# Third tile's gates: half by packed indirect adds, half by one-hot products; alternating heads; single gathers

## The reference, cut to what matters

```python
q = (xb @ w_query).reshape(T, PEER_HEADS, 2, PEER_HALF)             # 8 heads
s = einsum('thpk,hpnk->thpn', q, sub_keys)                          # 2 x 128 sub keys
top_s, top_i = top_k(s, 16)
cand_s = top_s[:, :, 0, :, None] + top_s[:, :, 1, None, :]
cand_i = top_i[:, :, 0, :, None] * 128 + top_i[:, :, 1, None, :]
best_s, best_pos = top_k(cand_s.reshape(T, 8, 256), 16)
idx = take_along_axis(cand_i.reshape(T, 8, 256), best_pos)          # 8 x 16 experts a token
gate = softmax(best_s)
act = gelu(einsum('td,thkd->thk', xb, expert_u[idx]))
out = einsum('thk,thkd->td', gate * act, expert_v[idx])
```

## Time and profile before

| | us |
|---|---|
| median of 3 runs | 2357.9 |
| lowest and highest | 2355.63, 2358.73 |
| profiled execution | 2360.8 |
| its span, first to last instruction | 2359.0 |
| busy: PE | 2306.6 |
| busy: DVE | 1470.8 |
| busy: ACT | 911.8 |
| busy: POOL | 779.1 |

### The profile page before, as it was taken

One profiled execution on the slowest core, in us unless ns is written; L12 is line 12 of the kernel. 1 busy time (PEld: TensorE's weight loads), 2 busy tenths in 40 slices (PEclk: granted clock), 3 DMA queues, 4 the chain that ended last, 5 costly groups with the idle time before them and its releaser, 6 DMA issues.

```text
span 2359.0 us, 29706 instructions
## 1 busy us (share of the span) xinstructions
PE 2306.6 (98%) x11108; PEld 1932.5 (82%) x11108; DVE 1470.8 (62%) x2879; ACT 911.8 (39%) x1342; POOL 779.1 (33%) x624
## 2 busy tenths in 40 slices
PE   8989899999999999999999999999999999999998
PEld 7879888888887888788888888888888788888887
DVE  4276568777435767667896553222222688888887
ACT  5346544333325445433333443222223333333333
POOL 0030011211000000000087777778630665656540
PEclk9999999999999999999999999999999999999999
DMA  6212057885222222333466558766666899999993
GB/s 231 82 45 63 1 166 237 291 275 192 98 98 85 86 72 63 119 103 101 125 137 159 121 121 226 193 143 145 147 210 217 288 369 370 373 379 378 356 391 107
DMA packets 205596, 434.21 MB, mean 184 GB/s; under 512 B 54176, under 2 KB 104368, under 8 KB 205072
## 3 DMA queue, kind: packets, MB, share of 16 engines
q1 hardware_dynamic: 81840, 251.79, 31.1%
q0 software_dynamic: 72848, 119.73, 18.7%
q10 hardware_dynamic: 50768, 60.82, 7.7%
HBM read 369.22 MB, written 63.05 MB: 183 GB/s over the span
## 4 chain that ended last, share of the span: by engine, by line
PE 94%; DVE 3%; ACT 1%; issue 1%; another core or an unknown queue 0%; DMA 0%; POOL 0%; ACTq 0%; DVEq 0%; POOLq 0%
PE PS L281 28%; PE PS L283 28%; PE PS L282 28%; PE PS L2346 1%; PE PS L2464 1%; PE PS L2278 1%; PE PS L2198 1%; PE PS L2266 1%; PE PS L2442 1%; PE PS L2123 1%; PE PS L2132 0%; DVE WL L276 0%; PE PS L2094 0%; PE PS L2232 0%
## 5 line engine op out<-in xcount | busy, mean ns | idle before, releaser
L276 DVE TENSOR_TENSOR WL<-RAW,WH 128x1024 fp32r<-128x1024 f32 (+1 forms) x414 | 505.4, 1222 | 687.3 <-ACT WH L270 658.6
L281 PE MATMUL PS<-HH,WH 128*128 128x512 f32 x1696 | 667.4, 394 | 6.5 <-DVE HL L513 4.6
L283 PE MATMUL PS<-HH,WL 128*128 128x512 f32 x1696 | 660.8, 390 | 0.0
L282 PE MATMUL PS<-HL,WH 128*128 128x512 f32 x1696 | 660.7, 390 | 0.0
L270 ACT ACTIVATE WH<-RAW 128x1024 fp32r<-128x1024 f32 (+1 forms) x414 | 435.6, 1054 | 445.8 <-PE PS L283 350.3
L942 POOL DMA_INDIRECT gates<-A,PLACE x256 | 420.2, 1641 | 316.6 <-DVE PLACE L1907 186.2
L281 PEld LDWEIGHTS PS<-HH,WH 128*128 128x128 f32 x1696 | 318.9, 188 | 75.1 <-issue 6.5
L283 PEld LDWEIGHTS PS<-HH,WL 128*128 128x128 f32 x1696 | 318.7, 188 | 67.0
L282 PEld LDWEIGHTS PS<-HL,WH 128*128 128x128 f32 x1696 | 318.9, 188 | 65.0 <-issue 1.0
L281 PE MATMUL PS<-WH,WGH 128*128 128x512 f32 x768 | 300.0, 391 | 2.1 <-DVE WGL L1968 1.0
L283 PE MATMUL PS<-WH,WGL 128*128 128x512 f32 x768 | 299.6, 390 | 2.4 <-issue 2.4
(11 more groups left out here) (375 smaller groups left out, 2640.1 us busy)
## 6 DMA issues: line engine op xcount, KB each, us to landing
RAW<-in_peer_u SPq DMA_DIRECT2D x128, 512.0 KB
RAW<-in_peer_v SPq DMA_DIRECT2D x128, 512.0 KB
A<-in_w_ada POOLq DMA_DIRECT2D x48, 512.0 KB, 4.8
A<-gates ACTq DMA_DIRECT2D x32, 768.0 KB
A<-acts ACTq DMA_DIRECT2D x32, 768.0 KB
RAW<-in_ffn_up SPq DMA_DIRECT2D x44, 512.0 KB
gates<-A POOLq DMA_DIRECT2D x16, 1024.0 KB, 6.9
acts<-GATE SPq DMA_DIRECT2D x64, 256.0 KB
```

The lines of the kernel that those rows point to most:

```text
L276: nc.vector.tensor_tensor(WLr[:, slot(c), 0:w], RAW[:, slot(c), 0:w], WH[:, slot(c), 0:w], ALU.subtract).then_inc(sem("low_done"), 1)
L281: nc.tensor.matmul(out, L[0], R[0], start=first, stop=False)
L282: nc.tensor.matmul(out, L[0], R[1], start=False, stop=False)
L283: return nc.tensor.matmul(out, L[1], R[0], start=False, stop=last)
```

## The change

`PACKED = 64` tokens of tile 2 now take the way of the adds, 64 that of the one-hot products.

- Tile 2 also gets addresses (`THIRD`) and gates. POOL packs them by four small DMAs from 64 partitions x 128 picks to 128 partitions x 64 picks (partition p + 64 holds the second eight picks of each head of token p), waits for them, and needs 64 indirect adds of 128 addresses for these 64 tokens. So there are 320 adds instead of 256. The zeroed columns grow from 256 to 320 (`ZW`).
- One-hot groups fall from 16 to 8 (`NG8`), and the staging tile and its store to half.
- Heads of tile 0, 1 and 2 alternate: tile 1 starts two rounds after tile 0, the packed half two rounds after tile 1. The packing stands before the fifth round.
- ACT's wait for the adds and its first loads of gates move from `QU - 6` to `QU - 3`, and include the third count.
- In the last stage POOL gathers 12 activations first and then one activation behind each row, five picks ahead; `final_w` is loaded at the 33rd row.
- SP stores the last activations one behind each of the first seven `peer_v` loads, instead of three so and four together.
- In two of the norms `root_of_rows` of tile 2 comes after the last tile's second half.
- Some semaphores are merged under other names.

```diff
+PACKED = P // 2
+ZW = NP * P + PACKED
+NG8 = (P - PACKED) // 8
...
+ACTS_AHEAD = 5
...
                 first_half(link, PS[:, 2 * t, :], 0)
-                root_of_rows(act, link, tag, 2)
                 rows_multiplied(act, tag, t + 1)
                 second_half(link, PS[:, 2 * t + 1, :], 0, product_sq[:, t:t + 1], product_rstd[:, t:t + 1], "product_root")
+                root_of_rows(act, link, tag, 2)
...
                 load((c0 + QU + v, 0, 0), peer_v[v])
-                if v < 3:
+                if v < 7:
                     keep_acts(P - 7 + v)
-                if v == 3:
-                    for k in range(P - 4, P):
-                        keep_acts(k)
...
-            for t in range(NP):
-                pool.wait_ge(sem("gates_listed"), t + 1)
-                for u in range(PICKS):
-                    if u >= TOPK and u % TOPK == 0:
-                        pool.wait_ge(sem(f"gates_placed{t}"), 16 * u)
-                    pool.indirect_dma_start(out=gate_list, out_offset=bass.IndirectOffsetOnAxis(ap=PLACE[:, t, u:u + 1], axis=0),
-                                            in_=SHARES[:, t, u:u + 1], in_offset=None, compute_op=ALU.add)\
+            def pack():
+                pool.wait_ge(sem("gates_listed"), NP + 1)
+                for dst, src in ((PACKED_AT, THIRD), (PACKED_SHARES, SHARES[:, NP])):
+                    for half in range(2):
+                        ps = slice(PACKED * half, PACKED * half + PACKED)
+                        pool.dma_start(dst[ps, :].rearrange("p (h k) -> p h k", h=PH),
+                                       src[0:PACKED, :].rearrange("p (h k) -> p h k", h=PH)[:, :, 8 * half:8 * half + 8])\
+                            .then_inc(sem("picks_packed"), 16)
+                pool.wait_ge(sem("picks_packed"), 64)
+
+            def add_head(t, h):
+                n, at, shares = (TOPK, PLACE[:, t], SHARES[:, t]) if t < NP else (TOPK // 2, PACKED_AT, PACKED_SHARES)
+                if h == 0 and t < NP:
+                    pool.wait_ge(sem("gates_listed"), t + 1)
+                if h > 0:
+                    pool.wait_ge(sem(f"gates_placed{t}"), 16 * n * h)
+                for u in range(n * h, n * h + n):
+                    pool.indirect_dma_start(out=gate_list, out_offset=bass.IndirectOffsetOnAxis(ap=at[:, u:u + 1], axis=0),
+                                            in_=shares[:, u:u + 1], in_offset=None, compute_op=ALU.add)\
                         .then_inc(sem(f"gates_placed{t}"), 16)
+
+            for r in range(PH + 4):
+                if r == 4:
+                    pack()
+                for t in range(NP + 1):
+                    if 0 <= r - 2 * t < PH:
+                        add_head(t, r - 2 * t)
...
-            pick_acts(0)
-            pool.dma_start(ROW[:, :], dr["final_w"].partition_broadcast(P)).then_inc(sem("row_landed"), 16)
-            pick_acts(1)
+            for u in range(SLOTS + ACTS_AHEAD):
+                pick_act(u)
             for u in range(SLOTS, PICKS):
                 pick_row(u)
-                if u % 8 == 7 and u // 8 + 2 < PICKS // 8:
-                    pick_acts(u // 8 + 2)
+                if u + ACTS_AHEAD < PICKS:
+                    pick_act(u + ACTS_AHEAD)
+                if u == PICKS // 4:
+                    pool.dma_start(ROW[:, :], dr["final_w"].partition_broadcast(P)).then_inc(sem("row_landed"), 16)
...
-                if p == QU - 6:
+                if p == QU - 3:
                     for t in range(NP):
                         act.wait_ge(sem(f"gates_placed{t}"), 16 * PICKS)
+                    act.wait_ge(sem(f"gates_placed{NP}"), 16 * PICKS // 2)
...
                 token = con("token")[:, t:t + 1].to_broadcast([P, PICKS])
-                if t < NP:
-                    nc.vector.scalar_tensor_tensor(PLACE[:, t], EXPERT, float(DW), token, ALU.mult, ALU.add)\
+                if t < ND:
+                    place = PLACE[:, t] if t < NP else THIRD
+                    nc.vector.scalar_tensor_tensor(place, EXPERT, float(DW), token, ALU.mult, ALU.add)\
                         .then_inc(sem("gates_listed"), 1)
...
-                for c in range(8 * n, 8 * n + 8):
+                for c in range(PACKED + 8 * n, PACKED + 8 * n + 8):
```

More of the change, by code:

```diff
@@ L51 @@
 NP = ND - 1
-ZW = NP * P
-NG8 = P // 8
+PACKED = P // 2
+ZW = NP * P + PACKED
+NG8 = (P - PACKED) // 8
 PICKS = PH * TOPK
@@ L778, in build @@
         SHARES = A[:, 21760:22144].rearrange("p (t u) -> p t u", t=ND)
-        STG = A[:, 0:16384].rearrange("p (i t) -> p i t", i=P)
+        STG = A[:, 0:8192].rearrange("p (i t) -> p i t", i=P)
+        THIRD = over("A", "THIRD", 8192, PICKS, U32)
+        PACKED_AT = over("A", "PACKED_AT", 8320, PICKS // 2, U32)
+        PACKED_SHARES = A[:, 8384:8448]
         OHA = A[:, 16384:18432].rearrange("p (r n) -> p r n", r=16)
@@ L951, in pick_row, with pick_act @@
                     .then_inc(sem(f"row_picked{u % SLOTS}"), 16)
[L953 to L961, removed]
+            def pick_act(u):
+                if u % 8 == 0:
+                    wait(pool, "rows_summed", u - 15)
+                pool.indirect_dma_start(out=AG[:, u:u + 1], out_offset=None, in_=act_list,
+                                        in_offset=bass.IndirectOffsetOnAxis(ap=A_AT[:, u:u + 1], axis=0))\
+                    .then_inc(sem(f"acts_picked{u // 8 % 2}"), 16)
+            pool.wait_ge(sem("gates_listed"), NT)
             pool.wait_ge(sem("gates_stored"), 16)
@@ L1079, in _ @@
                     act.wait_ge(sem("maxima_taken_off"), 1)
-                    nc.scalar.activation(E4, E4, ACT.Exp).then_inc(sem("late_exp"), 1)
+                    nc.scalar.activation(E4, E4, ACT.Exp).then_inc(sem("exps_taken"), 1)
                     act.wait_ge(sem("maxima_taken_off"), 2)
-                    nc.scalar.activation(lbt[:, 4:12], lbt[:, 4:12], ACT.Exp).then_inc(sem("late_exp"), 1)
+                    nc.scalar.activation(lbt[:, 4:12], lbt[:, 4:12], ACT.Exp).then_inc(sem("exps_taken"), 1)
                 if s - 1 in PTC_AT:
@@ L1279, in _ @@
                         act.wait_ge(sem("maxima_taken_off"), 2 + t + 1)
-                        nc.scalar.activation(BV[:, t % 2], BV[:, t % 2], ACT.Exp).then_inc(sem("best_exp"), 1)
+                        nc.scalar.activation(BV[:, t % 2], BV[:, t % 2], ACT.Exp).then_inc(sem("exps_taken"), 1)
                 if p == LIST_AT:
@@ L1562, in _ @@
                 if s == 27:
-                    dve.wait_ge(sem("late_exp"), 1)
+                    dve.wait_ge(sem("exps_taken"), 1)
                     for t in range(NT):
@@ L1573, in _ @@
                 if s == 29:
-                    dve.wait_ge(sem("late_exp"), 2)
+                    dve.wait_ge(sem("exps_taken"), 2)
                     link(nc.vector.tensor_tensor(lbt[:, 0:4], lbt[:, 4:8], lbt[:, 8:12], ALU.add))
@@ L1893, in listed @@
             def listed(t):
-                dve.wait_ge(sem("best_exp"), t + 1)
+                dve.wait_ge(sem("exps_taken"), 2 + t + 1)
                 n1, n2 = N12[:, t % 2, 0], N12[:, t % 2, 1]
@@ L1902, in listed @@
                     last.then_inc(sem("list_ready"), 1)
-                    return
                 link(nc.vector.scalar_tensor_tensor(EXPERT, n2, float(P), n1, ALU.mult, ALU.add))
                 token = con("token")[:, t:t + 1].to_broadcast([P, PICKS])
-                if t < NP:
-                    nc.vector.scalar_tensor_tensor(PLACE[:, t], EXPERT, float(DW), token, ALU.mult, ALU.add)\
+                if t < ND:
+                    place = PLACE[:, t] if t < NP else THIRD
+                    nc.vector.scalar_tensor_tensor(place, EXPERT, float(DW), token, ALU.mult, ALU.add)\
                         .then_inc(sem("gates_listed"), 1)
@@ L1911, in listed @@
                     nc.vector.scalar_tensor_tensor(V_AT, n1, float(P), n2, ALU.mult, ALU.add)\
-                        .then_inc(sem("picks_listed"), 1)
+                        .then_inc(sem("gates_listed"), 1)
             def shifted(t):
```

## The result

| | before | after |
|---|---|---|
| median, us (7 runs each) | 2358.04 | 2367.23 |
| lowest and highest | 2355.63, 2361.98 | 2363.07, 2373.31 |
| profiled execution, us | 2360.8 | 2363.07 |
| its span | 2359.0 | 2360.8 |

The ratio is 1.0032 with a 95% interval of 1.0021 to 1.0044: slower, by 5 to 10 us. The forecast was 2379.1: the right side and inside the range, but +21 where +9 was measured.

What follows compares the result with a forecast made beforehand. PE was taken to bound the kernel, with POOL's longer add stream delaying the last stage: +25.9 + 3.4 - 6.8 - 1.3 = +21.2 us on the median of 2357.9 gives 2379.1, range 2347 to 2412.

Steps and rivals of the forecast that it cites:

- T: Theory tested by the runs: the end of POOL's adds sets the start of the last stage, one to one.
- VectorE's missing wait: Sign in the norm transitions: no 0.66 us wait before VectorE's line 462 in the trace after.
- the period of 1.99: Sign in POOL's stream: 320 adds with a mean period near 1.99 us; under 1.92 the prediction is wrong.
- One-hot products: PE in the query stage: 8 of 16 one-hot groups go, at 1.78 us each, -14.2 us.
- The stream: POOL's indirect adds in the query stage: 320 x 1.990 = 636.8 us, plus 12 for landing waits and 10 for packing.
- Rival (c): POOL's stream: landing waits hid the gaps, so alternating heads gains nothing; +40 us more, 2419; chance 0.12.
- Rival (b): POOL's stream: VectorE stretches the adds, fewer one-hot rows speed them; 29 us less, -8, 2350; chance 0.08.
- Landing and loads: Start of the last stage: last add lands 3.0 us after its end, then 12 us of loads until PE starts.
- +25.9: PE's start of the last stage moves from 1821.0 to 1846.9 us, the 14.2 saved on one-hot products included.
- Restart: PE at the start of the last stage: reduced clock after standing for 40 us, +3.4 us.
- Single gathers: POOL in the last stage: one act beside each row spreads the gathers and removes the stall near 1862, -6.8 us.
- The norms: Transitions at 351 and 730 us: squares before tile 2's root_of_rows remove VectorE's wait, -1.3 us.

Runs made afterwards that it cites:

- e3: Changed kernel with 32 of its 64 packed adds left out, so its output is incomplete: 2339.03 us, 0.9937 of before.
- e7: Changed kernel with its tiles' adds one tile after the other instead of alternating heads: 2415.38 us, 1.0257 of before.
- e4: Changed kernel with 32 instead of 64 tokens by packed adds, 96 by one-hot products: 2346.41 us, 0.9967 of before.
- e1: Kernel before, unedited, run again for a second trace: 2352.76 us.
- e6: Kernel before with only the change's last-stage POOL order (single activation gathers, later final_w load): 2354.46 us, 0.9994 of before.
- e5: Kernel before with only the heads of its two tiles alternating: 2357.91 us in one execution.
- e8: Changed kernel with POOL's seven first row gathers held until the first group of activations landed: 2362.7 us, 1.0029 of before.
- e2: Changed kernel, unedited, measured and traced again: 2366.5 us, 1.0046 of before.
- e9: Changed kernel with reordered heads, a later wait for packing, row gathers held back and first row sum two chunks later: 2345.99 us, 0.9954 of before.

## Why the prediction was right and wrong

**The mechanism** was right: POOL's adds bound the query stage's end, ScalarE's wait passes that on, PE stands, the clock falls. T is shown from both sides, by e3 (stream 61 shorter: the stall gone) and e7 (stream 46 longer: 47 more idle). Of the signs that the prediction named, the 128 one-hot records, the late last add, ScalarE's wait, the half clock and VectorE's missing wait are there; PE's idle is not (25.4 us, forecast 30 to 45), nor the period of 1.99. The time moved the way that was forecast, but by 9 us instead of 21.

**One-hot products, -14.2.** Right: 14.4 in e3, 7.2 for half of them in e4.

**The stream, 658.5 us from the first add to the last add's end; measured 640.3.** The step that failed is "320 x 1.990 = 636.8". Cut at the waits, the adds took 618.5 us, 1.933 each. The price of 1.990 spread six gaps (17.1 us) over the adds as if they were a property of an add; without them and the landing waits the 256 adds of before took 1.92 each. The gaps belong to the tile-after-tile order: present in every trace with it (before, e1, e6, e7), always at the same adds, absent in every trace with alternating heads, e5 among them, where nothing else was changed. Rival (c) had the sign of this wrong: alternation does not expose gaps, it removes them. Rival (b) named the other part of the surplus; the mean of an add stayed at 1.63 to 1.65 us with all the one-hot rows or half of them, so what it promised did not come. Adds beside a busy VectorE are slower in rows 2, but no run varied VectorE's load where the lists are made. The four landing waits cost 9.6 (12 summed), the packing 12.2 (10 summed).

**Landing and loads, 3 + 12; measured 1.6 + 17.0.** The seven row gathers cost more than the 3 given to them. Without them the same path takes 9.8 (e8), so the gathers are 7 of the 17: 5 because the first activations reach VectorE later, 2 because ScalarE is held in the issue of its third pair of loads.

Together: -18.2 - 1.4 + 5.0 = -14.6, and +25.9 becomes the +11.3 of the table.

**Restart, +3.4.** 3.1 in the trace.

**Single gathers, -6.8.** Wrong. It took one stall of one execution for a cost of the kernel. The prediction had noted that the profiled run lay 2.9 us over the median, and used it only to shift the sum; it was a hint that the trace held something unusual. With this term gone the last stage costs +2.5 to +3.4 instead of -3.4, as the table shows against e1.

**The norms, -1.3.** Half shown: in the trace after, VectorE's line 464 (462 before) has no idle before it where rows 10 had 1.3, and from the first padding transpose to the first product the first of the two transitions takes 8.32 us (344.69 to 353.01) instead of 9.09 (348.05 to 357.14); in the second PE's wait for that line is also 0.76 shorter. That makes 1.5. No run had this edit alone.

**The balance.** Forecast +21.2. From the undisturbed traces: +11.3 (stage) + 3 (last stage) - 1.5 (norms) = +13; the medians say +9.2 and, in e2's series, +11.4. Two errors of opposite sign, 14.6 too much in the stage and some 6.5 too little in the last, left 8; the other 2 to 4 us between the traces and the medians are not accounted for. So it was luck that the error of the stream did not show in full. That the two first profiles differ by less than 3 us is luck too: the first trace of before held 8 us of it in its last stage, and ahead of the first add three short stretches of half clock, near 168, 267 and 738 us, where the changed kernel's trace had one, near 987. Each cost 1.7; with the norms' 1.5 the two more make the 4.9 us between the first adds, 1173.4 and 1168.6. So 13 - 8 - 3.4 = 1.6 is left of the cost, and the two spans differ by 1.8.

## What to carry to other kernels

Before moving work from the bounding engine to a queue that is off the path, add up the queue and compare it with when its result is asked for: here 70 us of slack, and what alternating gained, were spent on 64 adds of 1.93 us and the packing, and moving half as many (e4) gained 9 us where moving all of them cost 9 to 11. When a mean holds a few long gaps, find out what they are tied to before scaling it, and when one trace shows a stall that a change is to remove, take a second trace first. Once a stream is the bound, each small wait in it is worth its full length (e9), and what is issued right behind it counts too: holding back seven gathers of the next stage shortened the way from the loads to PE by 7 us, but they were missed later (e8).

## What the runs showed of the hardware

- With heads in sequence POOL's stream had gaps of 1.9 to 4.1 us before the same adds, 128 adds apart (61, 114, 121, then 189, 242, 249, and in e7 317), in four traces; with alternating heads none in eight. What makes them is open. In e7 the seventh comes 128 adds after the fourth although the packing and the end of a tile lie between. Neither the data (the addresses are the same in e5) nor the number of adds alone explains it; no run tried anything but the order.
- The issue of a load can hold ScalarE for long. The first pair of 768 KB loads took 0.9 us to issue; the third took 3.3 in the kernel before, 3.6 with the row gathers held back (e8), and 11.6 in the changed kernel with the row gathers in flight (DMA share 1.00 to 1.04).
- An idle of 25 us on PE cost 3.1 us of half clock behind it, one of 72 us 3.0 (e7), and one of 4.5 us was still followed by 5 us at 0.50 (1815 to 1820 in e9).
